# Narrow weights as the stationary side of three small projections in a two-layer decoder kernel

## The chip, the cores and the metric

The kernel runs on one core of one Trainium2 chip. The metric is the device time of one execution in microseconds (us), median of several runs. A change of about 0.2% (3.2 us) is what a measurement of this kernel can tell from no change.

## What is computed

Two decoder layers over 256 tokens of width 1024, all in float32. Layer 0 mixes with a forgetting attention, layer 1 with a gated sparse attention, and each is followed by a mixture of 64 experts. Three of its projections are narrow: they multiply the 256 normed and modulated tokens by a weight of 1024 x 16, 1024 x 48 or 1024 x 64.

```python
# forgetting attention, layer 0: 16 columns
log_f = jax.nn.log_sigmoid((proj[..., 3 * hd:] + b_f).astype(jnp.float32))
cum = jnp.cumsum(log_f, axis=1)
logits = logits + (cq.transpose(0, 2, 1)[..., None] - cum_k[:, :, None, :])
# sparse attention, layer 1: 48 columns
gates = jax.nn.sigmoid(proj[..., hd:] + b_gate).reshape(B, S, N_HEADS_B, 3)
o = gates[..., 0:1] * o_cmp + gates[..., 1:2] * o_sel + gates[..., 2:3] * o_win
# router, both layers: 64 columns
scores = jax.nn.sigmoid(jnp.matmul(h, w_router, preferred_element_type=jnp.float32))
_, top_e = lax.top_k(scores + b_router.astype(jnp.float32), TOP_K)
top_s = jnp.take_along_axis(scores, top_e, axis=-1)
top_w = top_s / jnp.sum(top_s, axis=-1, keepdims=True) * ROUTED_SCALE
```

## The kernel before

Each engine has its own list of instructions, written out by hand, and the lists meet at semaphores. SyncE streams all large weights, in units of 1 MiB, through a ring of 14 slots in a fixed order; it issues a unit when the slot's last user is done. TensorE works through the stages in order: the first conditioning vectors, the projections of layer 0 (`qkv`), its attention, the output projection (`out_a`), the experts of layer 0, then the key/value stage, the compression, the queries (`q`), the attention and the experts of layer 1. TensorE never skips ahead: an instruction that waits holds back all that stand behind it.

Before each projection, `pe_turn_rows` (L395) transposes the normed tokens (L404), and ScalarE and VectorE write the modulated tokens to `uT`, with the 1024 features in 8 chunks of 128 partitions and the 256 tokens along the row (L426, L434). `pe_modulated` (L410) waits for all eight chunks.

A normal projection unit (`pe_rows_unit`, L440) takes 128 tokens of `uT` as the stationary side and 256 weight columns as the moving side: 8 chunks times 2 token tiles are 16 matmuls. The three narrow projections do the same with 16, 48 or 64 moving columns:

```python
for t in range(NT):          # L865, the router; alike at L1379 and L1521
    for k in range(KC):
        mm = pe_.matmul(PS[:, Y0, t * N_EXP:(t + 1) * N_EXP], uT[:, k, t * P:(t + 1) * P],
                        w_router[:, k, :], start=(k == 0), stop=(k == KC - 1))
```

So each is 16 matmuls, and the result has tokens in partitions. A float32 matmul stands in the trace as two matmul records with a weight load each; a float32 transpose stands there as one.

- **Forget gate** (L1381). It is the first product of layer 0. VectorE's `forget_gate(step)` (L1701) and two ScalarE activations (Exp L1591, Ln L1594) turn it into log f, in five steps spread over the first units of the `qkv` loop (L1413). TensorE sums it over tokens after unit 2 (L1390 to L1392) and transposes the sums after unit 3 (L1398). `pe_rows_unit` of unit 0 (L446) stands right behind the forget matmuls.
- **Head gates** (L1523). The products of layer 1 ahead of the four `q` units (L446). VectorE adds the bias (L1854), ScalarE takes the sigmoid (L1667); the result is used after the queries.
- **Router** (L867, in `pe_moe`, both layers). Behind it stand `pe_gate` (L552, two matmuls of 512 columns that spread the layer's gate vector) and the shared expert's 32 matmuls (L875), then 16 transposes (L885), and only then the ranking (L890), which needs VectorE's mask of the chosen experts (L1066 to L1069). ScalarE takes the sigmoid of the scores from the PSUM accumulators (L1016).

Of the kernel before, what the change touches and what calls it, by code (L numbers as in the profile page):

```python
# [24 lines left out]
ALU = mybir.AluOpType  # L25
# [121 lines left out]
def build(nc, a, out):  # L147
    with ExitStack() as ctx:
# [40 lines left out]
        bias_f = sb("bias_f", [P, H])  # L189
        bias_gate = sb("bias_gate", [P, 3 * H])  # L190
# [7 lines left out]
        gates = sb("gates", [P, NT, 3 * H])  # L198
        small = sb("small", [P, 96])
# [62 lines left out]
        fg = [cut(F0 + 768 + 32 * i, [32]) for i in range(5)]  # L262
# [104 lines left out]
        ROUTING_SEMS = ["router_out", "scores_ready", "mask_ready", "ranks_out", "unranked_ready", "unranked_turned",  # L367
# [70 lines left out]
        KV_BANK = [0, 1, 2, 0, 1, 6]  # L438

# [351 lines left out]

        ranks_ps = PS[:, Y0 + 1, 0:NT * N_EXP].rearrange("p (t e) -> p t e", t=NT)
# [65 lines left out]
        def pe_moe(pe_, layer):  # L858
# [63 lines left out]
            pe_.wait_ge(routing["place_ready"], layer + 1)  # L922
            for kind in range(2):
# [86 lines left out]
        def act_moe(done, layer):  # L1010
# [5 lines left out]
            done(act.activation(scores.rearrange("p t e -> p (t e)"), PS[:, Y0, 0:NT * N_EXP], ACT.Sigmoid),  # L1016
                 routing["scores_ready"])
# [39 lines left out]
        def dve_moe(done, layer):  # L1057
# [7 lines left out]
            for t in range(NT):  # L1065
                done(dve.tensor_tensor(chosen_by[:, t, :], scores[:, t, :], bias_router[:, layer, :], ALU.add))  # L1066
# [3 lines left out]
            done(dve.tensor_tensor(scores, scores, routed, ALU.mult))  # L1070
# [194 lines left out]
        def _(pool):  # L1265
# [9 lines left out]
            for dst, src in ((gain_qa, "qnorm_a"), (gain_ka, "knorm_a"), (gain_qb, "qnorm_b"),  # L1275
                             (bias_f, "b_f_a"), (bias_gate, "b_gate_b")):
                pool.dma_start(dst[:, :], rows(a[src][0])).then_inc(params, 16)
            for i in range(3):
# [93 lines left out]
        def _(pe_):  # L1372
# [6 lines left out]
            for t in range(NT):  # L1379
                for k in range(KC):  # L1380
                    mm = pe_.matmul(PS[:, 6, t * H:(t + 1) * H], uT[:, k, t * P:(t + 1) * P], w_forget[:, k, :],  # L1381
                                    start=(k == 0), stop=(k == KC - 1))
            mm.then_inc(sem("forget_out"), 1)

            def forget_sums():
                lf = fg[4].rearrange("p (t h) -> p t h", t=NT)
                sums = PS[:, 6, 2 * H:4 * H].rearrange("p (t h) -> p t h", t=NT)
                pe_.wait_ge(sem("logf_ready"), 1)
# [24 lines left out]
            for j in range(12):  # L1413
# [107 lines left out]
            for t in range(NT):  # L1521
                for k in range(KC):
                    mm = pe_.matmul(PS[:, 6, t * 3 * H:(t + 1) * 3 * H], uT[:, k, t * P:(t + 1) * P],  # L1523
                                    w_gates[:, k, :], start=(k == 0), stop=(k == KC - 1))
            mm.then_inc(sem("gates_out"), 1)
# [36 lines left out]
        def _(act):  # L1562
# [21 lines left out]
            for j in range(8):  # L1584
# [4 lines left out]
                if j == 0:  # L1589
                    act.wait_ge(sem("forget_abs"), 1)  # L1590
                    done(act.activation(fg[2], fg[1], ACT.Exp, scale=-1.0), sem("forget_exp"))  # L1591
                elif j == 1:
                    act.wait_ge(sem("forget_1p"), 1)
                    done(act.activation(fg[3], fg[2], ACT.Ln), sem("forget_ln"))  # L1594
# [71 lines left out]
            act.wait_ge(sem("gates_biased"), 1)  # L1666
            done(act.activation(gates[:, :, :], gates[:, :, :], ACT.Sigmoid), sem("gates_ready"))  # L1667
# [15 lines left out]
        def _(dve):  # L1683
# [15 lines left out]
            z, az, ez, lnz, logf = fg  # L1699

            def forget_gate(step):  # L1701
                if step == 0:
                    dve.wait_ge(sem("forget_out"), 1)
                    done(dve.tensor_tensor(z.rearrange("p (t h) -> p t h", t=NT),
                                           PS[:, 6, 0:2 * H].rearrange("p (t h) -> p t h", t=NT),
                                           bias_f[:, :].unsqueeze(1).to_broadcast([P, NT, H]), ALU.add))
                    done(dve.tensor_scalar(az, z, -1.0, None, ALU.mult))
                    done(dve.tensor_tensor(az, az, z, ALU.max), sem("forget_abs"))
                elif step == 1:
                    dve.wait_ge(sem("forget_exp"), 1)  # L1710
                    done(dve.tensor_scalar(ez, ez, 1.0, None, ALU.add), sem("forget_1p"))
                    done(dve.tensor_scalar(z, z, 0.0, None, ALU.min))
                elif step == 2:
                    dve.wait_ge(sem("forget_ln"), 1)
                    done(dve.tensor_tensor(logf, z, lnz, ALU.subtract), sem("logf_ready"))
                elif step == 3:
                    dve.wait_ge(sem("cum_out"), 1)
# [282 lines left out]
```

## Time and profile before

| | |
|---|---|
| median of 3 runs | 1584.86 us |
| range of these runs | 1583.45 to 1586.05 us |
| the profiled execution | 1586.27 us, span 1584.4 us, clock 0.957 |
| TensorE (PE) busy | 1480.9 us, 93% |
| VectorE (DVE) busy | 417.6 us, 26% |
| ScalarE (ACT) busy | 280.8 us, 18% |
| moved by DMA | 512.38 MB, mean 323 GB/s |

The span runs from the first to the last instruction; the execution's own time is 1.9 us longer. PE busy counts matmuls, PEld weight loads, which run beside them. PEclk is the TensorE clock that was granted, as a share of 2.4 GHz: 1.00 is 2.4 GHz, 0.50 is 1.2 GHz. "Idle before" names what an engine waited for.

### The profile page before, as it was taken

What the parts mean: (1) busy time and instruction counts of PE and PEld (TensorE: products, weight loads), DVE (VectorE), ACT (ScalarE), POOL (GpSimd) and SP (SyncE); (2) the same over time, 40 slices, a digit from 0 to 9 for tenths busy, and PEclk for the clock granted to TensorE, in tenths of its full rate; (3) what the DMA queues carried; (4) which work ended last, traced back from release to release, by engine and by line L of the source; (5) the groups of instructions that cost most, each with busy time, mean ns of one, the idle gap of its engine ahead of it and who ended that gap; (6) DMA issues with size and microseconds to landing.
All of it is one profiled execution on the core that took longest, in us unless ns stands there. A gap on an engine that the chain in (4) does not pass through costs nothing.

```text
span 1584.4 us, 21198 instructions
## 1 busy us (share of the span) xinstructions
PE 1480.9 (93%) x8561; PEld 888.8 (56%) x8561; DVE 417.6 (26%) x969; ACT 280.8 (18%) x549; POOL 31.4 (2%) x81
## 2 busy tenths in 40 slices
PE   4999988999999999999798868789999999999998
PEld 2777777644555444454376757676455454544443
DVE  0466432111111111111367247522111111111111
ACT  2211332111111111111212215421111111111110
POOL 4000001000000000000000000001000000000000
PEclk9999987999999999999999768889999999999999
DMA  9967602399999999999999810031999999999996
GB/s 342 413 265 309 255 27 87 135 376 422 421 421 422 374 421 420 421 420 422 417 404 384 360 53 1 1 113 34 368 421 422 421 420 375 422 420 421 420 421 264
DMA packets 71315, 512.38 MB, mean 323 GB/s; under 512 B 8176, under 2 KB 8400, under 8 KB 9264
## 3 DMA queue, kind: packets, MB, share of 16 engines
q1 hardware_dynamic: 69984, 508.59, 78.5%
q0 software_dynamic: 800, 1.28, 0.4%
q8 instruction: 69, 1.13, 0.3%
q10 hardware_dynamic: 432, 1.13, 0.2%
q14 instruction: 30, 0.25, 0.0%
HBM read 509.92 MB, written 1.05 MB: 322 GB/s over the span
## 4 chain that ended last, share of the span: by engine, by line
PE 87%; DVE 5%; ACT 3%; issue 2%; DMA 1%; DVEq 0%; ACTq 0%
PE PS L823 23%; PE PS L446 13%; PE PS L813 12%; PE PS L831 12%; PE PS L846 11%; PE PS L875 2%; PE PS L616 2%; PE PS L404 2%; PE PS L469 2%; PE PS L483 1%; DMA h<-in_x 1%; PE PS L913 1%; PE PS L867 1%; DVE acc L527 1%; PE PS L586 1%
## 5 line engine op out<-in xcount | busy, mean ns | idle before, releaser
L823 PE MATMUL PS<-ring,scratch 128*32 128x512 f32 (+2 forms) x2048 | 367.8, 594 | 1.4 <-ACT scratch L1030 1.4
L823 PEld LDWEIGHTS PS<-ring,scratch 128*32 128x32 f32 (+2 forms) x2048 | 118.8, 127 | 243.7 <-issue 241.9
L446 PE MATMUL PS<-ring,uT 128*128 128x256 f32 x960 | 224.3, 395 | 2.9 <-ACT uT L417 1.8
L813 PEld LDWEIGHTS PS<-scratch,u 128*128 128x128 f32 x1664 | 190.8, 192 | 39.5 <-issue 37.6
L446 PEld LDWEIGHTS PS<-ring,uT 128*128 128x128 f32 x960 | 189.2, 199 | 31.8 <-ACT uT L417 2.6
L813 PE MATMUL PS<-scratch,u 128*128 128x128 f32 x1664 | 199.6, 278 | 1.4 <-ACT scratch L1030 1.4
L1154 DVE TENSOR_TENSOR scratch<-PS,gate_row 128x512 f32<-128x512 f32 x104 | 72.0, 692 | 464.1 <-PE PS L831 464.1
L831 PE MATMUL PS<-ring,scratch 128*32 128x512 f32 (+2 forms) x1024 | 189.3, 596 | 1.2 <-DVE item_first_i L1139 1.2
L846 PE MATMUL PS<-scratch 128*128 128x512 f32 x416 | 187.3, 593 | 0.0
L1038 ACT ACTIVATE scratch<-PS 128x256 f32<-128x256 f32 x52 | 20.0, 384 | 675.7 <-PE PS L823 675.7
L831 PEld LDWEIGHTS PS<-ring,scratch 128*32 128x32 f32 (+2 forms) x1024 | 56.8, 126 | 125.5 <-issue 123.8
L846 PEld LDWEIGHTS PS<-scratch 128*128 128x128 f32 x416 | 75.0, 190 | 76.3 <-issue 74.6
L1147 DVE TENSOR_TENSOR scratch<-scratch,PS 128x256 f32<-128x256 f32 x52 | 21.9, 422 | 337.5 <-ACT scratch L1038 337.5
L1030 ACT ACTIVATE scratch<-PS 128x512 f32<-128x512 f32 x104 | 62.1, 597 | 162.9 <-PE PS L813 162.9
L527 DVE SCALAR_TENSOR_TENSOR acc<-ring,cond,acc 128x256 f32<-128x256 f32 x168 | 81.5, 485 | 6.0
L483 PE MATMUL PS<-ring,scratch 128*32 128x256 f32 x512 | 42.5, 460 | 12.2 <-DVE scratch L1687 6.8
L616 PE MATMUL PS<-scratch,uT 128*128 128x65 f32 x288 | 38.4, 284 | 12.2 <-ACT uT L639 12.2
L616 PEld LDWEIGHTS PS<-scratch,uT 128*128 128x128 f32 x288 | 35.0, 196 | 19.3 <-ACT uT L639 17.3
L404 PE MATMUL PS<-ident,u 128*128 128x128 f32 x112 | 25.2, 419 | 18.4 <-ACT u L721 16.1
L647 ACT ACTIVATE scratch<-scratch,stats 128x128 f32<-128x128 f32 (+1 forms) x96 | 35.7, 443 | 19.0 <-DVE stats L666 19.0
L469 PE MATMUL PS<-four_rows,acc 128*128 128x1 f32 x128 | 22.8, 283 | 15.1 <-ACT acc L497 14.8
L404 PEld LDWEIGHTS PS<-ident,u 128*128 128x128 f32 x112 | 22.9, 227 | 20.4 <-issue 17.7
(306 smaller groups left out, 918.6 us busy)
## 6 DMA issues: line engine op xcount, KB each, us to landing
ring<-in_w_exp SPq DMA_DIRECT2D x384, 1024.0 KB, 15.5
ring<-in_w_ada_units SPq DMA_DIRECT2D x56, 1024.0 KB, 11.7
ring<-in_w_in_a_units SPq DMA_DIRECT2D x12, 1024.0 KB, 8.5
ring<-in_w_cmp_units SPq DMA_DIRECT2D x8, 1024.0 KB, 9.4
ring<-in_w_sh_units SPq DMA_DIRECT2D x6, 1024.0 KB, 16.2
ring<-in_w_kv_b_units SPq DMA_DIRECT2D x6, 1024.0 KB, 19.6
ring<-in_w_o_a_units SPq DMA_DIRECT2D x4, 1024.0 KB, 7.2
ring<-in_w_in_b_units SPq DMA_DIRECT2D x4, 1024.0 KB, 17.1
```

The lines of the kernel that those rows point to most:

```text
L404: mm = pe_.transpose(PS[:, b, (k % 2) * SEQ + t * P:(k % 2) * SEQ + (t + 1) * P], src[:, t, k * P:(k + 1) * P], ident[:, :])
L446: mm = pe_.matmul(PS[:, bank, t * UC:(t + 1) * UC], lhs[:, k, t * P:(t + 1) * P], w[:, k, :], start=(k == 0), stop=(k == KC - 1))
L469: return [pe_.matmul(PS[:, ADA_COLUMNS, c0 + c:c0 + c + 1], part[:, c * P:(c + 1) * P], rows, start=True, stop=True) for c in range(2)]
L483: mm = pe_.matmul(PS[i:i + 32, ada_parts_bank(j), 0:UC], cond_cols[:, k, :], w[:, k, :], start=(k < 4), stop=(k >= 4))
L527: done(dve.scalar_tensor_tensor(out=sums, in0=w[:, k, :], scalar=cond[:, k:k + 1], in1=sums, op0=ALU.mult, op1=ALU.add), ada_products_read ...
L616: mm = pe_.matmul(PS[:, 6 + b % 2, hd * (DH + 1):(hd + 1) * (DH + 1)], pT[:, n * P:(n + 1) * P], values(br, kt, 4 * g + hd), start=(kt == ...
L813: mm = pe_.matmul(PS[:, bank, i * w:(i + 1) * w], u[:, t, k * P:(k + 1) * P], hot[:, t, :], start=(t == 0), stop=(t == NT - 1))
L823: mm = pe_.matmul(PS[i * w:(i + 1) * w, GU, :], x[:, kk, i * w:(i + 1) * w], gate_and_up, start=(kk == 0), stop=(kk == KC - 1))
L831: mm = pe_.matmul(PS[i * w:(i + 1) * w, Y0 + half, :], hT[:, j, i * w:(i + 1) * w], down[:, j, half * 512:(half + 1) * 512], start=(j == 0 ...
L846: mm = pe_.matmul(OUT[t][:, half * 512:(half + 1) * 512], hot_wT[0:rows, t * P:(t + 1) * P], y_rows[0:rows, half * 512:(half + 1) * 512], ...
L1030: act.activation(x_pair[g % 2][:, 4 * half:4 * half + 4, :].rearrange("p k s -> p (k s)"), PS[:, gather_bank(g, half), :], ACT.Copy).then_ ...
L1154: dve.tensor_tensor(y_rows[:, half * 512:(half + 1) * 512], PS[:, Y0 + half, :], gate_row[:, half * 512:(half + 1) * 512], ALU.mult).then_ ...
```

## The change

The three narrow projections swap sides: each chunk of the narrow weight is stationary and all 256 tokens move, so that 8 matmuls stand in place of 16, and the result has the 16, 48 or 64 features in partitions and tokens along the row. Bias, sigmoid and log-sigmoid work in that layout, and two small transposes per projection bring the finished result back to tokens in partitions. The biases of the two gates are loaded as columns. For the router the transposed scores are read from PSUM by VectorE.

```diff
+        def pe_narrow(pe_, w, bank, lhs, columns, turned):
+            for k in range(KC):
+                mm = pe_.matmul(PS[0:columns, bank, 0:SEQ], w[:, k, :], lhs[:, k, :], start=(k == 0), stop=(k == KC - 1))
+            mm.then_inc(turned, 1)
+        def pe_narrow_rows(pe_, src, rows):
+            for t in range(NT):
+                mm = pe_.transpose(rows[:, t, :], src[:, t * P:(t + 1) * P], ident[0:src.shape[0], 0:src.shape[0]])
+            return mm
...
-            for t in range(NT):
-                for k in range(KC):
-                    mm = pe_.matmul(PS[:, Y0, t * N_EXP:(t + 1) * N_EXP], uT[:, k, t * P:(t + 1) * P],
-                                    w_router[:, k, :], start=(k == 0), stop=(k == KC - 1))
-            mm.then_inc(routing["router_out"], 1)
+            pe_narrow(pe_, w_router, Y0, uT, N_EXP, routing["router_out"])
             pe_gate(pe_, 2 * layer + 1)
+            pe_.wait_ge(routing["sigmoids"], layer + 1)
+            pe_narrow_rows(pe_, narrow_T[E64, :], scores_ps).then_inc(routing["scores_ready"], 1)
...
-            done(act.activation(scores.rearrange("p t e -> p (t e)"), PS[:, Y0, 0:NT * N_EXP], ACT.Sigmoid),
-                 routing["scores_ready"])
+            done(act.activation(narrow_T[E64, :], PS[E64, Y0, 0:SEQ], ACT.Sigmoid), routing["sigmoids"])
...
+            def forget_turn():
+                pe_.wait_ge(sem("logf_ready"), 1)
+                pe_narrow_rows(pe_, logits_f, narrow_rows(6, SEQ, H)).then_inc(sem("logf_turned"), 1)
...
                 if j == 2:
+                    forget_turn()
+                elif j == 3:
                     forget_sums()
-                elif j == 3:
+                elif j == 4:
                     forget_rows()
...
             for j in range(4):
                 pe_rows_unit(pe_, AT["q", j], j, uT)
+                if j == 0:
+                    pe_.wait_ge(sem("gates_active"), 1)
+                    pe_narrow_rows(pe_, narrow_T[0:3 * H, :], narrow_rows(6, SEQ, 3 * H)).then_inc(sem("gates_turned"), 1)
...
-            act.wait_ge(sem("gates_biased"), 1)
-            done(act.activation(gates[:, :, :], gates[:, :, :], ACT.Sigmoid), sem("gates_ready"))
+            act.wait_ge(sem("gates_out"), 1)
+            done(act.activation(narrow_T[0:3 * H, :], PS[0:3 * H, 6, 0:SEQ], ACT.Sigmoid, bias=bias_gate[:, :]),
+                 sem("gates_active"))
...
-                    done(dve.tensor_scalar(az, z, -1.0, None, ALU.mult))
-                    done(dve.tensor_tensor(az, az, z, ALU.max), sem("forget_abs"))
+                    done(dve.tensor_scalar(logits_f, PS[0:H, 6, 0:SEQ], bias_f[:, :], None, ALU.add))
+                    done(dve.scalar_tensor_tensor(out=softplus_f, in0=logits_f, scalar=-1.0, in1=logits_f,
+                                                  op0=ALU.mult, op1=ALU.max), sem("forget_abs"))
...
+                elif step == 3:
+                    dve.wait_ge(sem("logf_turned"), 1)
+                    done(dve.tensor_copy(logf_rows, PS[:, 6, SEQ:SEQ + NT * H]), sem("logf_copied"))
```

TensorE's list at the router, before. `router_loaded` is the weight's DMA, `modulated_*` the eight chunks of `uT`, `slot_loaded` a unit of the ring:

```order
L404 MATMUL PS<-ident,u 128x128 x15
L867 MATMUL PS<-scratch,uT 128x64 [waits router_loaded,modulated_dve,modulated_act]
L867 MATMUL PS<-scratch,uT 128x64 x15
L552 MATMUL PS<-scratch,ones 128x512 [waits gate_diag_ready]
L552 MATMUL PS<-scratch,ones 128x512
L875 MATMUL PS<-uT,ring 128x256 [waits slot_loaded6]
L875 MATMUL PS<-uT,ring 128x256 x7
```

And now, with the line numbers of the changed kernel (L445 is the narrow matmul, L453 the transpose back, L568 the gate, L890 the shared expert):

```order
L406 MATMUL PS<-ident,u 128x128 x15
L445 MATMUL PS<-uT,scratch 64x256 [waits router_loaded,modulated_dve,modulated_act]
L445 MATMUL PS<-uT,scratch 64x256 x7
L568 MATMUL PS<-scratch,ones 128x512 [waits gate_diag_ready]
L568 MATMUL PS<-scratch,ones 128x512
L453 MATMUL PS<-ident,narrow_T 128x64 [waits sigmoids]
L453 MATMUL PS<-ident,narrow_T 128x64
L890 MATMUL PS<-uT,ring 128x256 [waits slot_loaded6]
L890 MATMUL PS<-uT,ring 128x256 x7
```

Eight matmuls stand in place of 16, and behind the gate TensorE now waits for ScalarE's sigmoids ahead of two transposes; the shared expert is queued behind that wait.

TensorE's list at the head gates, now:

```order
L406 MATMUL PS<-ident,u 128x128 x15
L445 MATMUL PS<-uT,w_gates 48x256 [waits cmp_v_read,modulated_dve,modulated_act]
L445 MATMUL PS<-uT,w_gates 48x256 x7
L462 MATMUL PS<-ring,uT 128x256 [waits slot_loaded1]
L462 MATMUL PS<-ring,uT 128x256 x15
L453 MATMUL PS<-ident,narrow_T 128x48 [waits gates_active]
L453 MATMUL PS<-ident,narrow_T 128x48
L462 MATMUL PS<-ring,uT 128x256 [waits slot_loaded2]
```

Here the wait stands behind the first `q` unit of 16 matmuls (L462 now, L446 before).

## Rows read from the trace of the kernel before

**Rows 1.** The page: span, busy time, and the chain by engine

```profile
span 1584.4 us, 21198 instructions
...
PE 87%; DVE 5%; ACT 3%; issue 2%; DMA 1%; DVEq 0%; ACTq 0%
```

**Rows 2.** Waits: who waited for whom, us in total, times, longest us

```profile
SPq L1215 <- PE PS L831: 432.1, 48, 10.4
SPq L1215 <- PE PS L446: 260.6, 14, 112.2
```

**Rows 3.** Timeline, TensorE, forget gate: start us, us, engine line op, count [idle before]

```profile
42.27 3.65 PE L404 MATMUL PS<-ident,u 128*128 128x128 f32 x16
47.06 6.98 PE L1381 MATMUL PS<-w_forget,uT 128*128 128x16 f32 x32 [1.14 <-ACT uT L426]
53.89 9.08 PE L446 MATMUL PS<-ring,uT 128*128 128x256 f32 x32
62.90 1.07 PE L483 MATMUL PS<-ring,scratch 128*32 128x256 f32 x16
```

**Rows 4.** Timeline, TensorE, 58 to 62.9 us

```profile
57.44 5.53 PE L446 MATMUL PS<-ring,uT 128*128 128x256 f32 x24
```

**Rows 5.** Timeline, TensorE, router of layer 0 and shared expert

```profile
256.98 3.65 PE L404 MATMUL PS<-ident,u 128*128 128x128 f32 x16 [4.83 <-ACT u L721]
261.76 7.06 PE L867 MATMUL PS<-scratch,uT 128*128 128x64 f32 x32 [1.14 <-ACT uT L426]
268.61 3.73 PE L552 MATMUL PS<-scratch,ones 128*128 128x512 f32 x4
272.13 14.34 PE L875 MATMUL PS<-uT,ring 128*128 128x256 f32 x64
286.31 1.91 PE L885 MATMUL PS<-ident,uT 128*128 128x128 f32 x16
288.05 0.33 PE L890 MATMUL PS<-scratch,before 128*128 128x64 f32 x2
```

**Rows 6.** Timeline, TensorE, router of layer 1 and shared expert

```profile
1064.46 7.06 PE L867 MATMUL PS<-scratch,uT 128*128 128x64 f32 x32 [1.14 <-ACT uT L426]
1071.31 3.73 PE L552 MATMUL PS<-scratch,ones 128*128 128x512 f32 x4
1074.83 14.05 PE L875 MATMUL PS<-uT,ring 128*128 128x256 f32 x64
1088.72 1.47 PE L885 MATMUL PS<-ident,uT 128*128 128x128 f32 x12
```

**Rows 7.** Timeline, TensorE, head gates and the four q units

```profile
885.06 5.04 PE L1523 MATMUL PS<-w_gates,uT 128*128 128x48 f32 x32 [1.14 <-ACT uT L426]
889.91 29.92 PE L446 MATMUL PS<-ring,uT 128*128 128x256 f32 x128
```

**Rows 8.** Timeline, TensorE, spreading of the compressed heads in layer 1

```profile
940.93 7.19 PE L1545 MATMUL PS<-scratch 64*128 64x512 f32 x8 [0.53 <-ACT scratch L1675]
```

**Rows 9.** Windows, TensorE: stretch, its us, PE busy (x), PEclk, DMA share, GB/s

```profile
54.00:57.90 3.90, 3.90 (x11) 1.00 1.01 416
...
884.00:887.20 3.20, 2.14 (x20) 1.00 1.00 417
887.30:893.80 6.50, 6.50 (x23) 0.50 1.01 420
...
261.80:268.60 6.80, 6.80 (x32) 0.50 0.01 2
268.80:272.60 3.80, 3.80 (x7) 0.50 0.01 2
273.10:286.00 12.90, 12.90 (x61) 1.00 0.25 83
...
941.00:948.00 7.00, 7.00 (x8) 0.50 0.00 0
```

**Rows 10.** Timeline, ScalarE and VectorE, behind the router of layer 0

```profile
268.86 0.28 ACT L1016 ACTIVATE scratch<-PS 128x128 f32<-128x128 f32 x1 [6.72 <-PE PS L867]
...
270.93 0.29 DVE L1069 TENSOR_TENSOR scratch<-scratch 128x128 f32<-128x128 f32 x1
```

**Rows 11.** Groups by line and shape: busy us, mean ns | idle before

```profile
L1038 ACT ACTIVATE scratch<-PS 128x256 f32<-128x256 f32 x26 | 10.0, 384 | 337.9 <-PE PS L823 337.9
...
L527 DVE SCALAR_TENSOR_TENSOR acc<-ring,cond,acc 128x256 f32<-128x256 f32 x168 | 81.5, 485 | 6.0
```

More of the change, by code:

```diff
@@ L261, in build @@
         forget_queries = cut(F0 + 512, [SEQ])
-        fg = [cut(F0 + 768 + 32 * i, [32]) for i in range(5)]
+        logf_rows = cut(F0 + 768, [NT * H])
+        logits_f, softplus_f = narrow_T[0:H, :], cut(S0 + 2304, [SEQ])[0:H]
         def of_queries(rows):
@@ L922, in pe_moe @@
             pe_.wait_ge(routing["place_ready"], layer + 1)
+            pe_.wait_ge(routing["raw_scores_read"], layer + 1)
             for kind in range(2):
@@ L1378, in _ @@
             pe_.wait_ge(params, 16 * N_PARAMS)
[L1379 to L1383, printed above, removed]
+            pe_narrow(pe_, w_forget, 6, uT, H, sem("forget_out"))
+            def forget_turn():
+                pe_.wait_ge(sem("logf_ready"), 1)
+                pe_narrow_rows(pe_, logits_f, narrow_rows(6, SEQ, H)).then_inc(sem("logf_turned"), 1)
             def forget_sums():
-                lf = fg[4].rearrange("p (t h) -> p t h", t=NT)
-                sums = PS[:, 6, 2 * H:4 * H].rearrange("p (t h) -> p t h", t=NT)
-                pe_.wait_ge(sem("logf_ready"), 1)
+                lf = logf_rows.rearrange("p (t h) -> p t h", t=NT)
+                sums = narrow_rows(6, SEQ + NT * H, H)
+                pe_.wait_ge(sem("logf_copied"), 1)
                 pe_.wait_ge(consts, 1)
@@ L1520, in _ @@
             pe_.wait_ge(sem("cmp_v_read"), 1)
[L1521 to L1525, printed above, removed]
+            pe_narrow(pe_, w_gates, 6, uT, 3 * H, sem("gates_out"))
             for j in range(4):
                 pe_rows_unit(pe_, AT["q", j], j, uT)
+                if j == 0:
+                    pe_.wait_ge(sem("gates_active"), 1)
+                    pe_narrow_rows(pe_, narrow_T[0:3 * H, :], narrow_rows(6, SEQ, 3 * H)).then_inc(sem("gates_turned"), 1)
             pe_turn_rows(pe_, q_rows, (sem("q_normed"), 4), "q")
@@ L1713, in forget_gate @@
                 elif step == 2:
                     dve.wait_ge(sem("forget_ln"), 1)
-                    done(dve.tensor_tensor(logf, z, lnz, ALU.subtract), sem("logf_ready"))
+                    done(dve.scalar_tensor_tensor(out=logits_f, in0=logits_f, scalar=0.0, in1=softplus_f,
+                                                  op0=ALU.min, op1=ALU.subtract), sem("logf_ready"))
                 elif step == 3:
+                    dve.wait_ge(sem("logf_turned"), 1)
+                    done(dve.tensor_copy(logf_rows, PS[:, 6, SEQ:SEQ + NT * H]), sem("logf_copied"))
+                elif step == 4:
@@ L1717, in forget_gate @@
                     dve.wait_ge(sem("cum_out"), 1)
-                    sums = PS[:, 6, 2 * H:4 * H].rearrange("p (t h) -> p t h", t=NT
-                                                           ).unsqueeze(2).to_broadcast([P, NT, 2, H])
+                    sums = narrow_rows(6, SEQ + NT * H, H).unsqueeze(2).to_broadcast([P, NT, 2, H])
                     done(dve.tensor_copy(of_queries(cum), sums))
                     done(dve.tensor_scalar(of_keys(cum_keys), sums, -1.0, None, ALU.mult), sem("cum_ready"))
-                elif step == 4:
+                elif step == 5:
@@ L1988 @@
                                      given["norm_ffn"][1], given["c"])
-    for name in ("x", "positions", "b_f_a", "qnorm_a", "knorm_a", "pe_cmp_k", "pe_cmp_v", "w_cmp_k2", "w_cmp_v2",
-                 "knorm_b", "b_gate_b", "qnorm_b", "b_router"):
+    for name in ("x", "positions", "qnorm_a", "knorm_a", "pe_cmp_k", "pe_cmp_v", "w_cmp_k2", "w_cmp_v2",
+                 "knorm_b", "qnorm_b", "b_router"):
         laid_out[name] = given[name]
+    laid_out["b_f_column"] = given["b_f_a"].reshape(H, 1)
+    laid_out["b_gate_column"] = given["b_gate_b"].reshape(3 * H, 1)
     for name, value in laid_out.items():
```

35 lines of the change are left out of this document (17 added, 18 removed).

## The prediction

> **What bounds the kernel now.** I read the page first. TensorE makes up 87% of the chain that ended last, and issue, DMA and the other engines share the rest [rows 1]. So what TensorE's list loses, the kernel loses, unless a load is late. The waits say that it is not: the queue that loads the weights waited for TensorE, 432 us behind the expert matmuls and 261 us behind the projections [rows 2]. Around the router DMA moves nearly nothing, since the ring is full there (share 0.01 [rows 9]). After it, loads and matmuls both follow from this point, so a gain ahead of the experts moves the whole rest and is not given back to DMA. The same holds at the forget gate and the head gates, where TensorE waited for `uT` and for no load [rows 3, 7].
>
> Then I read TensorE's own timeline at the four places, from start to start. Forget gate: 53.89 - 47.06 = 6.83 us, and the unit behind it 9.01 us [rows 3]. Router of layer 0: 6.85 us, gate 3.52 us, shared expert 14.18 us [rows 5]; of layer 1: 6.85, 3.52 and 13.89 us [rows 6]. Head gates: 4.85 us, the four `q` units about 29.9 us [rows 7].
>
> **Two levels of the clock.** The length of a matmul depends on the clock, so the windows come next. Layer 0's router and gate ran at a granted clock of 0.50, which is 1.2 GHz; from 273 us it was 1.00 [rows 9]. At the head gates it was 1.00 until 887.2 us and then 0.50 until about 894, so the first `q` unit paid for it. The column is no guide at the forget gate. It reads 1.00, but the first 8 records of 256 columns behind it took (57.44 - 53.89)/8 = 0.44 us each, and the later 24 took 5.46/24 = 0.23 [rows 3, 4]. The gate's 512-column records give 3.52/4/2 = 0.44 us for 256 columns at 0.50 [rows 5]. At the full clock it is 13.89/64 = 0.217 us [rows 6]. So the first 11 us of layer 0's products start at the low level as well.
>
> **What the change does to the narrow matmuls.** Before, 16 matmuls are 32 records, each with a 128-column weight load and at most 64 moving columns, so the load sets their pace: 6.85/32 = 0.214 us at the low clock [rows 5] and 4.85/32 = 0.152 us at the mostly full clock [rows 7]. Now 8 matmuls are 16 records with 256 moving columns. That is 16 x 0.44 = 7.0 us low and 16 x 0.217 = 3.5 us full. So at the low level nothing is gained, although half of the matmuls are gone, and at the full level 1.4 us of 4.85 are.
>
> The Trainium skill, page "TensorE: Matmul & The Clock Gate", section "LDWEIGHTS (loading the stationary operand)", gives P/1.2 ns for P columns, which is 107 ns for 128. By that, an estimate, the 32 loads of before take 3.4 us, as long as the 16 new records, and the swap gains nothing even at the full clock. The 0.152 us of the head gates stands against it, and the row decides.
>
> **What the low clock does.** Everything hangs on whether the narrow matmuls bring the clock up or keep it up. Two rows of the same length stand against each other. The gate's records (128 rows and 128 columns of the array, 512 moving columns) began at the low level at 268.6 and 1071.3 us, and the clock was up some 4 us later [rows 5, 6, 9]. L1545 is as dense, 8 records of 0.90 us, but fills 64 of the 128 rows; after 7.2 us of it the clock still read 0.50 [rows 8, 9]. The new matmuls use all 128 rows, but 16, 48 or 64 columns. No row shows columns left empty at the low level without neighbours beside them. I take the nearest row, L1545, which also leaves at least half of the array unused. So in my forecast the narrow matmuls do not raise the clock, and gate and shared expert behind them come as before.
>
> **The sum.** Forget gate 7.04 - 6.83 = +0.2 us. Each router 7.04 - 6.85 = +0.2. Head gates: full until 887.2 us, 2.14/0.217 = 10 records, then 6 x 0.44 = 2.6, together 4.8 against 4.85: 0. The `q` units then pay for the low stretch as before. Bounds of a narrow block: 3.5 us (all full) and 7.0 us (all low).
>
> Transposes back, two at each of four places: a record costs 1.91/16 = 0.12 us at the full clock [rows 5] and 3.65/16 = 0.23 low [rows 3]. Forget gate and head gates full, 0.24 each; the routers low, right behind the gate, 0.46 each: +1.4 us. Bounds: 1.0 us in all if all are full, and 1.4 + 4 x 0.8 = 4.6 us if TensorE had to wait for every ScalarE answer.
>
> That answer is costed at nothing. ScalarE began 0.25 us after the last router matmul and took 0.28 us [rows 5, 10]; with 256 columns it is 0.38 [rows 11], so the sigmoids are there some 0.8 us after the narrow matmuls, under the gate's 3.5 us (1.7 at full clock). At the head gates the first `q` unit of 7 us covers it, at the forget gate a whole unit. Without that cover it costs up to 0.8 us a place, and the shared expert waits with it. Behind the router, VectorE's choice now starts up to 4 us later than before. Its mask was begun at 270.9 us and is needed at 288.0, so the shared expert covers that. If it did not, the ranking would be late next [rows 5, 10].
>
> VectorE's forget steps now work on 256 columns instead of 32, up to 0.49 us each [rows 11], with one step more, and sums and transposed sums come one unit later. All of it lies beside units of 9 to 10 us with eight units to come: 0, and 0.5 us where VectorE is the later one. The bias loads, the same number in smaller pieces, land long before 47 us: 0.
>
> Total: 0.2 + 0.2 + 0.2 + 0 + 1.4 = **+2.0 us**. Against the profiled execution that is 1586.3 + 2.0 = 1588.3 us. That execution lies 1.4 us over the median of 1584.86, so I forecast **1586.9 us**, within what can be told from no change.
>
> **Rival A, the narrow matmuls wake the clock (as L552 does).** Then the low stretch of about 4 us starts with them: 9 records of 0.44 and 7 of 0.217 are 5.5 us, and all behind is at the full clock. Forget gate: 5.5 + 32 x 0.217 = 12.4 against 15.84, -3.4 us. Router of layer 0: 5.5 + 1.74 + 13.89 = 21.1 against 24.55, -3.4; of layer 1 against 24.26, -3.1. Head gates: the clock never falls, 3.5 + 27.8 = 31.3 against 34.75, -3.5. All transposes at the full clock, +1.0. Together -12.4: 1572.5 us by the median. For it: L552, and that all 128 rows stream without a gap. Against it: L1545. The Trainium skill's page just named, section "The HAM clock gate (the "warmup" mystery)", says that activity releases the throttle and names no share of the array; by it this rival would be the forecast. Rows 8 do not follow it in that short form. Chance 38%. In between, with later rises, it gives -7 us.
>
> **Rival B, slower: the clock is already down when the head gates start.** Before, it was 1.00 at their start and fell 2 us in [rows 9]. If it is low at 885 us, the 16 records take 7.04 instead of 4.85 us, +2.2 us. If it also rises 4 us later in the `q` units, 9 records lose 0.22 each, +2.0. With the +2.0 of the forecast that is +6.2, 1591.1 us. It decides as soon as no high stretch reaches the head gates. For it: those matmuls use 48 of 128 columns, and the clock did fall in this place. Against it: the transposes ahead of them are untouched, and the clock came up behind those. Chance 8%.
>
> **Rival C, only the head gates gain.** Started at the full clock, 256 columns in a row may hold a level that they cannot raise: 4.85 - 3.5 = 1.4 us and about 1.9 us in the `q` units, against +2.0 elsewhere: -1.3, 1583.6 us. Still no change. Chance 7%.
>
> **How the numbers follow.** The forecast's own case has 47%, its own range 1584 to 1589.5 us: the transposes' bounds and the clock's falls elsewhere, such as one more or fewer low stretch of 1.7 us. Rival A lies at 1569 to 1577. The range must hold both: 1571 to 1589.5, which leaves out rival B, the low end of A and the high end of the waits. Faster by over 0.2% (3.2 us): A and some 3% of the others, 41%. Slower by over 0.2%: B and the forecast's case with stalls, 15%. Within 0.2%: 44%.
>
> **What would show it.** Forecast right: the narrow blocks at router and forget gate take 7 us, the gate behind the router still 3.5 us at 0.50, and the first `qkv` unit still about 9 us. Rival A: narrow blocks near 5.5 us, gate 1.7 us, first `qkv` unit 7 us, and no fall at the head gates. Any wait of the shared expert for the sigmoids shows a cost I set to nothing; so does VectorE's mask as the releaser of the ranking.

## Result and profile after

The changed kernel took 1575.4 us (median of 6 runs, 1571.4 to 1580.3), the kernel before 1584.6 us in the same job (6 runs, 1583.5 to 1586.1). The ratio is 0.9942, 95% interval 0.9923 to 0.9962: 9.2 us less, faster by more than 0.2%. The forecast of no change was wrong. The time lies in the range, near the 1572.5 us of rival A. The profiled execution of the changed kernel took 1571.4 us, the least of its six, and is 14.7 us shorter than that of before.

The page of the changed kernel, span and chain [rows 1]:

```profile
span 1569.7 us, 21088 instructions
...
PE 87%; DVE 6%; ACT 4%; issue 2%; DMA 1%; DVEq 0%; ACTq 0%
```

The mix of the chain is nearly the same, so the time went inside TensorE's own list. TensorE's timeline of the changed kernel at the four places, in the columns of [rows 3]. L445 is the narrow block, L462 a unit of 32 records, L568 the gate, L453 the transposes back, L890 the shared expert:

```profile
44.23 3.61 PE L445 MATMUL PS<-uT,w_forget 128*16 128x256 f32 x16 [1.14 <-ACT uT L428]
47.77 7.17 PE L462 MATMUL PS<-ring,uT 128*128 128x256 f32 x32
...
82.29 0.29 PE L453 MATMUL PS<-ident,narrow_T 16*128 16x16 f32 x2
...
249.14 3.65 PE L406 MATMUL PS<-ident,u 128*128 128x128 f32 x16 [4.83 <-ACT u L737]
253.93 5.46 PE L445 MATMUL PS<-uT,scratch 128*64 128x256 f32 x16 [1.14 <-ACT uT L428]
259.32 1.98 PE L568 MATMUL PS<-scratch,ones 128*128 128x512 f32 x4
261.24 0.34 PE L453 MATMUL PS<-ident,narrow_T 64*128 64x64 f32 x2
261.50 14.08 PE L890 MATMUL PS<-uT,ring 128*128 128x256 f32 x64
...
874.93 5.56 PE L445 MATMUL PS<-uT,w_gates 128*48 128x256 f32 x16 [1.14 <-ACT uT L428]
880.42 7.17 PE L462 MATMUL PS<-ring,uT 128*128 128x256 f32 x32
887.53 0.32 PE L453 MATMUL PS<-ident,narrow_T 48*128 48x48 f32 x2
```

Against [rows 3, 5, 7]: the forget gate's block fell from 6.83 to 3.54 us and the unit behind it from 9.01 to 7.11. The router's block went from 6.85 to 5.39 and the gate from 3.52 to 1.92. The head gates' block became longer, 5.49 instead of 4.85, but the first unit behind it is at full pace. Windows of the changed kernel show the clock under these blocks. Here and in the windows below the columns are the stretch, its us, the busy us (and instructions) of PE, PEld, DVE, ACT and POOL, then PEclk, DMA share and GB/s:

```profile
254.00:257.40 3.40, 3.40 (x9) 1.83 (x10) 0.96 (x1) 0.29 (x1) 0.00 (x0) 0.50 0.02 5
257.60:259.30 1.70, 1.70 (x8) 0.82 (x6) 0.00 (x0) 0.00 (x0) 0.00 (x0) 0.99 0.00 0
...
874.90:878.80 3.90, 3.87 (x10) 1.90 (x11) 0.00 (x0) 0.82 (x1) 0.00 (x0) 0.50 1.01 420
879.00:880.40 1.40, 1.40 (x7) 0.62 (x5) 0.00 (x0) 0.00 (x0) 0.00 (x0) 1.00 1.03 421
```

Both blocks began at 0.50 (1.2 GHz) and ended at 1.00 (2.4 GHz): 64 and 48 filled columns of the array did bring the clock up, during the block itself. That is rival A, and what the forecast ruled out.

Where the 14.7 us of the two profiles lie, from starts in TensorE's timeline. "Turn" is where a block's transposes of `u` begin:

| stretch | before, us | after, us | difference |
|---|---|---|---|
| start to forget gate | 47.06 | 44.23 | -2.8 |
| forget gate and first unit | 15.84 | 10.65 | -5.2 |
| to the turn that ends layer 0's attention | 152.8 | 155.6 | +2.8 |
| to the router block | 46.1 | 43.4 | -2.6 |
| router, gate, shared expert, layer 0 | 24.55 | 21.49 | -3.1 |
| experts, to the turn of layer 1 | 495.8 | 495.8 | 0 |
| to the head gates | 102.9 | 103.7 | +0.8 |
| head gates and `q` units | 38.9 | 38.0 | -0.9 |
| layer 1's attention | 94.6 | 93.1 | -1.5 |
| to the router block | 45.8 | 46.2 | +0.4 |
| router, gate, shared expert, layer 1 | 24.26 | 21.69 | -2.6 |
| rest | 495.7 | 495.8 | +0.1 |

The four changed places gave 11.8 us. The start gave 2.8 us that no step of the prediction names. The attention stages moved by -1.5 and +2.8 us, although the change puts nothing there but the forget gate's small steps beside the `qkv` units. Over the twelve profiles of this study that add nothing to it, layer 0's stretch took from 152.8 to 156.2 us, with old and with new blocks alike. The expert stages kept their time, so nothing was given back to DMA, as argued from [rows 2].

### The profile page after: what moved, and what is told of

Same layout as the page of the kernel before. It is cut to its first block, busy times and chain, and to the rows that moved or that the text cites. A ratio compares the mean times of both kernels' runs of the same rounds, so it can differ in the third digit from the quotient of the medians.

```text
span 1569.7 us, 21088 instructions
## 1 busy us (share of the span) xinstructions
PE 1467.1 (93%) x8505; PEld 868.6 (55%) x8505; DVE 423.5 (27%) x968; ACT 281.7 (18%) x549; POOL 31.5 (2%) x81
## 4 chain that ended last, share of the span: by engine, by line
PE 87%; DVE 6%; ACT 4%; issue 2%; DMA 1%; DVEq 0%; ACTq 0%
PE PS L840 23%; PE PS L462 13%; PE PS L830 12%; PE PS L848 12%; PE PS L863 11%; PE PS L632 2%; PE PS L890 2%; PE PS L406 2%; PE PS L485 1%; DVE acc L543 1%; PE PS L445 1%; PE PS L499 1%; DMA h<-in_x 1%; PE PS L928 1%; PE PS L619 1%
## 5 line engine op out<-in xcount | busy, mean ns | idle before, releaser
L462 PE MATMUL PS<-ring,uT 128*128 128x256 f32 x960 | 220.5, 390 | 3.1 <-ACT uT L419 1.9
L462 PEld LDWEIGHTS PS<-ring,uT 128*128 128x128 f32 x960 | 186.0, 196 | 31.7 <-ACT uT L419 2.6
L1053 ACT ACTIVATE scratch<-PS 128x256 f32<-128x256 f32 x52 | 19.9, 383 | 675.7 <-PE PS L840 675.7
## 6 DMA issues: line engine op xcount, KB each, us to landing
ring<-in_w_exp SPq DMA_DIRECT2D x384, 1024.0 KB, 15.6
```

What stands on the lines that cost most here:

```text
L462: mm = pe_.matmul(PS[:, bank, t * UC:(t + 1) * UC], lhs[:, k, t * P:(t + 1) * P], w[:, k, :], start=(k == 0), stop=(k == KC - 1))
```

## The experiments

All ratios are to the kernel before, run beside it on the same chip, with 95% intervals. A "low stretch" is one in which the granted clock was 0.50.

**The three places one by one.** Each kernel swaps one place alone and leaves the others as before. The edit, shown for the forget gate (the other two are cut out of the diff above in the same way):

```diff
-            for t in range(NT):
-                for k in range(KC):
-                    mm = pe_.matmul(PS[:, 6, t * H:(t + 1) * H], uT[:, k, t * P:(t + 1) * P], w_forget[:, k, :],
-                                    start=(k == 0), stop=(k == KC - 1))
-            mm.then_inc(sem("forget_out"), 1)
+            pe_narrow(pe_, w_forget, 6, uT, H, sem("forget_out"))
...
```

> Only the forget gate swaps sides; router and head gates are as before. Theory A (a dense stream of 256 columns through all 128 rows wakes the clock, however few columns of the array the weight fills): the narrow block takes 5.5 us where the clock is low at its start and 3.5 us where it is not, the first qkv unit 7.0 instead of 9.0 us, so 3.2 to 5.2 us faster than before. Theory B (my forecast: a weight of 16 columns does not wake it): the block takes 7.0 us, the unit 9.0 us, and the time is the same within 0.5 us. By theory A a narrow block is faster in some runs than in others, so the runs spread wider than those of before.

Measured: 1583.8 us, 12 runs, ratio 0.9992 (0.9979 to 1.0005).

> Only the head gates swap sides. Theory A: the clock no longer falls in the q units; 31.3 us instead of 34.75 us for gates and q units where the clock is up at their start (-3.3 us with the transposes), 33.5 us where it first has to rise (-1 us). Theory B: 4.8 us for the gates, the q units as before, 0.2 us slower.

Measured: 1582.3 us, 9 runs, ratio 0.9976 (0.9966 to 0.9986).

> Only the router swaps sides, in both layers. Theory A: narrow block 5.5 us, gate 1.8 to 1.9 us, shared expert 13.9 us in each layer, 3.0 us a layer and 6 us in all faster than before. Theory B: 7.0, 3.5 and 14.2 us, 1.3 us slower in all.

Measured: 1588.9 us, 12 runs, ratio 1.0015 (1.0001 to 1.0028).

And the whole change again in the same job:

> The whole change once more. If its parts act alone (theory A), the gain is the sum of those of the other three kernels of this job, within 1.5 us. If the profiled run of the change shown so far (the fastest of its six) owed its 14.7 us to where the clock rose and fell, this profile shows the same narrow blocks but other stretches of low clock elsewhere, and its gain lies near 9 us.

Measured: 1577.0 us, 6 runs, ratio 0.9937 (0.9922 to 0.9952).

Each place did locally what rival A says. TensorE's timeline of the forget gate alone:

```profile
47.49 3.61 PE L445 MATMUL PS<-uT,w_forget 128*16 128x256 f32 x16 [1.14 <-ACT uT L428]
51.03 7.17 PE L462 MATMUL PS<-ring,uT 128*128 128x256 f32 x32
```

and of the head gates alone:

```profile
884.50 3.62 PE L444 MATMUL PS<-uT,w_gates 128*48 128x256 f32 x16 [1.14 <-ACT uT L427]
...
895.16 0.32 PE L452 MATMUL PS<-ident,narrow_T 48*128 48x48 f32 x2
895.41 20.99 PE L461 MATMUL PS<-ring,uT 128*128 128x256 f32 x96
```

Forget gate with first unit: 10.65 us instead of 15.84. Head gates with `q` units up to the next turn: 36.1 us instead of 38.9, and here the block began at the full clock and no fall came. The router alone took 2.9 us off layer 0 (26.5 instead of 29.3 us from the turn to the end of the shared expert) and 2.7 off layer 1, and the kernel was still no faster than before: 3.3 us slower by the medians, with an interval that just leaves out no change. The three parts come to 1583.8 - 1585.7, 1582.3 - 1585.7 and 1588.9 - 1585.7: -1.9, -3.4 and +3.3 us, together -2.0, where the whole gives -8.7. **The parts do not add up.** Of the 6.7 us between them 2.8 belong to the start, which only the whole change moves: the forget block began at 46.9 to 47.5 us in the profiles of the three parts and at 44.3 in that of the whole. The remaining 3.9 us are hardly more than the intervals of the four ratios allow together (some 4 us, an estimate from their widths). The router alone is the clear case: 5.6 us gained at its two places, and none in the total.

**What moves is the clock elsewhere.** In the router-only profile the gains are lost in stages that the edit does not touch. Layer 1's attention took 101.1 us instead of 94.6, the head gates with `q` 40.8 instead of 38.9 (their block began low and took 6.83 us), layer 0's attention 156.1 instead of 152.8. The next pair asks whether the place of the work in time alone does this. One kernel is before with 0.55 us of unused matmuls behind layer 0's shared expert. The other is router-only with 2.86 us of them at that point, meant to let the rest of the program start as late as in before. The edit of the second:

```diff
+        def pe_keep_busy(pe_, n, bank=7, columns=248):
+            for _ in range(n):
+                pe_.matmul(PS[:, bank, 264:264 + columns], ones[:, :], causal[:, 0:columns], start=True, stop=True)
...
+            if layer == 0:
+                pe_keep_busy(pe_, 6)
+                pe_keep_busy(pe_, 1, columns=228)
```

> The kernel before, with 0.55 us of extra matmuls (332 columns, results unused) behind the shared expert of layer 0 and nothing else changed. In the router-only kernel the attention of layer 1 ran with a low stretch of the clock from 974.75 to 991.75 us and took 101.1 us from the end of the queries to its end, against 94.65 us before. Theory A (the low stretches depend on where a stage falls against the clock's own rhythm, and a gain upstream only moves them): moving all that follows by a fraction of a microsecond changes the time by other than 0.55 us, by 3 to 7 us where it brings the attention into the same position. Theory B (the swap itself harms something in the router-only kernel): 0.5 to 0.6 us slower than before, and the attention takes 94.7 us.

Measured: 1588.9 us, 11 runs, ratio 1.0013 (1.0003 to 1.0023), which is 2.5 us over before by the medians and 0.5 to 3.6 us by the interval.

> The router-only kernel, with 2.86 us of extra matmuls at the same place, so that all that follows starts where it does before the change. Theory A: the low stretch in the attention of layer 1 is gone, and although work was added the kernel is faster than the router-only one (1588.9 us), by 6.5 - 2.9 = 3.6 us or so. Theory B: 2.9 us slower than the router-only kernel.

Measured: 1583.5 us, 12 runs, ratio 0.9987 (0.9975 to 0.9999), with 2.9 us more work 5.4 us less than router-only by the medians (4.4 by the ratios, since the two come from two jobs). Windows of layer 1's attention, first router-only, then router-only with the added matmuls:

```profile
922.80:1023.90 101.10, 82.97 (x490) 67.71 (x490) 63.06 (x152) 42.16 (x92) 0.00 (x0) 0.71 0.00 1
974.80:991.70 16.90, 16.90 (x85) 15.40 (x86) 10.80 (x27) 6.82 (x15) 0.00 (x0) 0.50 0.00 1
```

```profile
922.70:1017.30 94.60, 75.13 (x491) 60.48 (x491) 63.02 (x152) 42.25 (x92) 0.00 (x0) 0.77 0.00 1
974.80:991.70 16.90, 15.34 (x138) 13.36 (x138) 15.60 (x39) 11.79 (x28) 0.00 (x0) 1.00 0.00 1
```

The same 490 matmuls start 0.1 us apart in the two profiles. With the clock at 0.50 between 974.8 and 991.7 us, 85 of them were done in that stretch, with it at 1.00, 138. That one low stretch is the 6.5 us. So this stage, in which TensorE is about 80% busy, has low stretches whose number changes although it starts at the same microsecond of the program. The second profile of the whole change has such a one, too, where the first took 93.1 us:

```profile
916.30:1017.50 101.20, 81.69 (x490) 66.29 (x490) 63.06 (x151) 42.70 (x92) 0.00 (x0) 0.72 0.00 1
```

This answers the question of the pair, and the answer is no: the place in time, counted from the program's start, does not decide alone. What is shown is that 2.86 us of added work left the router-only kernel faster, by 4.4 us by the ratios, whose intervals just part. Why is not shown. Its profile starts the rest 0.3 us earlier than the router-only one, in spite of the added work, because layer 0's attention had taken 3.3 us less ahead of it, so a part of the gain need not be the added matmuls' doing. For before with 0.55 us added, the attention kept its 94.7 us, and the loss came at the head gates, which began low (40.9 instead of 38.9 us). Its interval reaches down to the 0.55 us themselves, so it does not show that a small shift costs more than itself.

**Rows or columns.** This kernel is before, with the gate's four matmuls reading 64 rows instead of 128, as L1545 does:

```diff
+            rows = slice(0, 64 if i in (1, 3) else P)
-                mm = pe_.matmul(PS[:, half, :], ones[:, :],
-                                gate_diag[:, 4 * half:4 * half + 4, :].rearrange("p k c -> p (k c)"),
+                mm = pe_.matmul(PS[:, half, :], ones[rows, :],
+                                gate_diag[rows, 4 * half:4 * half + 4, :].rearrange("p k c -> p (k c)"),
```

> The kernel before, where the gate matmuls of both routers (L552) use 64 of 128 rows; half of the gate vector is left out of the output. If the filled rows decide whether a dense stream brings the clock up (my reading of L1545 against L552), the clock stays at 0.50 through the gate and comes up only some 4 us into the shared expert, which then takes 15.5 to 16 us instead of 13.9 to 14.2. If rows do not matter, gate and shared expert read as before, and something else kept the clock down behind L1545.

Measured: one run of 1622.4 us. This kernel leaves half of the gate vector out, so layer 1 routes otherwise, and the total says nothing. TensorE's timeline at the routers of both layers, and windows at that of layer 0:

```profile
270.12 3.78 PE L553 MATMUL PS<-scratch,ones 64*128 64x512 f32 x4
273.83 15.78 PE L876 MATMUL PS<-uT,ring 128*128 128x256 f32 x64
...
1072.26 3.78 PE L553 MATMUL PS<-scratch,ones 64*128 64x512 f32 x4
1075.97 15.78 PE L876 MATMUL PS<-uT,ring 128*128 128x256 f32 x64
```

```profile
270.20:273.80 3.60, 3.60 (x4) 1.09 (x4) 2.81 (x14) 0.28 (x1) 0.00 (x0) 0.50 0.01 2
274.00:277.20 3.20, 3.20 (x8) 2.57 (x9) 0.01 (x1) 1.02 (x1) 2.03 (x1) 0.50 0.00 0
277.50:289.40 11.90, 11.90 (x57) 10.46 (x56) 0.00 (x0) 1.88 (x2) 2.36 (x2) 1.00 0.26 89
```

With all rows the clock was up some 4 us after the gate began [rows 5, 9]. With half of them it stayed at 0.50 through the gate and 3.4 us into the shared expert, 7.1 us after the gate began, and the shared expert took 15.6 instead of 14.2 us. Layer 1's router repeats it: 15.6 instead of 13.9 us. So in these runs rows left empty kept a dense matmul from raising the clock, as at L1545, and columns left empty did not. L1545 was a good row, for another question. Only half of the rows was tried, no other share.

**Holding the clock up.** If the low stretches are the price, unused matmuls in front of the places should take it away. First the changed kernel with 10 of them ahead of each router's transposes and 14 ahead of layer 1's first ones, where TensorE waited anyhow:

```diff
+            pe_keep_busy(pe_, 10, 3)
             pe_.wait_ge(mix_added, 4)
...
```

> The changed kernel, with unused matmuls where TensorE waits ahead of the transposes: 10 of 248 columns (4.1 us) ahead of both routers and 14 (5.8 us) ahead of the key/value stage. If the dense stream through all rows is what brings the clock up, it never falls there: transposes 1.9 instead of 3.65 us (with about 1 us of that given back to the modulation of the tokens), narrow block 3.5 instead of 5.5, gate 1.7 instead of 1.9: 3 us a router, 1 us at the key/value stage, 6 to 7 us faster than the change, save for what the attention's low stretches take or give by their new position (up to 7 us either way).

Measured: 1564.5 us, 5 runs, ratio 0.9854 (0.9840 to 0.9867), 11 us under the change by the medians of two jobs and 13 to 14 by the ratios, where 6 to 7 was expected. One part of the miss is the stretch from the turn of layer 1 to the head gates: 99.7 instead of 103.7 us, where 1 us was expected. TensorE's timeline at layer 0's router, and then at the forget gate, where nothing was added:

```profile
251.74 1.94 PE L410 MATMUL PS<-ident,u 128*128 128x128 f32 x16 [0.65 <-ACT u L741]
254.85 3.64 PE L449 MATMUL PS<-uT,scratch 128*64 128x256 f32 x16 [1.17 <-ACT uT L432]
258.42 1.98 PE L572 MATMUL PS<-scratch,ones 128*128 128x512 f32 x4
```

```profile
44.45 5.89 PE L449 MATMUL PS<-uT,w_forget 128*16 128x256 f32 x16 [1.14 <-ACT uT L432]
50.27 7.17 PE L466 MATMUL PS<-ring,uT 128*128 128x256 f32 x32
```

Transposes 1.94 instead of 3.65 us, narrow block 3.57, gate 1.9. The forget gate's block took 5.82 us here, the unit behind it 7.11. Windows inside the block show the pace of the records. The clock's column reads 1.00 at this place in any case, as in [rows 9], so the pace must tell the level:

```profile
44.50:48.50 4.00, 4.00 (x10) 1.37 (x11) 3.36 (x11) 0.00 (x0) 0.00 (x0) 1.00 1.02 426
...
49.20:50.20 1.00, 1.00 (x6) 0.29 (x3) 0.70 (x2) 0.00 (x0) 0.00 (x0) 1.00 0.99 410
```

Some 0.44 us a record at first and 0.22 at the end (10.4 x 0.44 + 5.6 x 0.22 = 5.8): 16 filled columns woke the clock as well.

Then such matmuls in all the waits that had low stretches (2 a step of the compression, ahead of the `q` transposes and of the compressed probabilities, one a batch of both attentions), in the changed kernel and in before:

> The kernel with unused matmuls ahead of routers and key/value stage, and more of them where TensorE waits in the compression (2 a step), ahead of the queries' transposes (9), ahead of the compressed probabilities (11) and once in each batch of both attentions that reads two key tiles. If a dense stream holds the clock: no low stretch from 870 us to the end, some 4 us less at the compressed heads, 2 us each at the transposes and the compressed logits, no low stretch in either attention. 1553 us, give or take 5, and runs within 3 us of each other, since there is nothing left whose position matters.

Measured: 1553.8 us, 5 runs, ratio 0.9784 (0.9768 to 0.9800). This is the best kernel of the study, 32 us under before. Two parts of the expectation failed: the runs lie 6.1 us apart, not within 3, and the profile still has low stretches behind 870 us, of some 7 us at 909 and 10 us at 933 and 991.

> The same unused matmuls in the kernel before. With the clock held up in the attentions, the change's own gain is left: 1.4 us for each of four narrow blocks, 2.8 us at the load of x, less 1.0 us of transposes, and at the forget gate and the head gates what the old narrow matmuls cost by letting the clock fall (up to 2 us each). So 6 to 11 us slower than the same with the change. If the gain of the change lies in the attention's low stretches alone, the two are within 2 us.

Measured: 1562.0 us, 7 runs, ratio 0.9841 (0.9829 to 0.9854). So with the clock mostly held up in both, the change is worth 8.2 us, about what it gives without. The two profiles lie 15.8 us apart, but this one was the slowest of its seven runs. The two kernels show what the old block does by itself. TensorE's timeline at the head gates and windows of that place and of layer 1's router, in before with the added matmuls:

```profile
875.39 4.82 PE L1532 MATMUL PS<-w_gates,uT 128*128 128x48 f32 x32 [1.14 <-ACT uT L430]
```

```profile
875.50:877.50 2.00, 2.00 (x19) 2.00 (x20) 0.00 (x0) 0.68 (x1) 0.00 (x0) 1.00 0.97 406
878.00:880.00 2.00, 2.00 (x11) 2.00 (x11) 0.00 (x0) 0.00 (x0) 0.00 (x0) 0.50 1.00 414
1049.70:1051.60 1.90, 1.90 (x18) 1.90 (x18) 1.01 (x1) 0.83 (x1) 0.00 (x0) 1.00 0.00 0
1052.00:1054.00 2.00, 2.00 (x11) 2.00 (x11) 0.00 (x0) 0.00 (x0) 0.00 (x0) 0.50 0.00 0
```

and of the same head gates in the changed kernel with the added matmuls, its timeline:

```profile
866.78 3.65 PE L449 MATMUL PS<-uT,w_gates 128*48 128x256 f32 x16 [1.23 <-ACT uT L432]
870.37 7.17 PE L466 MATMUL PS<-ring,uT 128*128 128x256 f32 x32
```

The three old blocks of head gates and routers, now begun at 1.00, lost the clock 2.2 to 2.6 us in. In the new form all three kept it. From block to `q` turn, 38.9 against 36.1 us. From router block to the end of the shared expert, 22.5 against 19.7 in both layers.

**The first 2.8 us.** In the changed kernel `x` is there sooner, and TensorE's first blocks start sooner with it. ScalarE's timeline, first of before, then of the changed kernel:

```profile
19.29 1.06 ACT L691 ACTIVATE u<-h 128x1024 f32<-128x1024 f32 x1 [11.39 <-DMA h<-in_x]
```

```profile
16.80 1.06 ACT L707 ACTIVATE u<-h 128x1024 f32<-128x1024 f32 x1 [8.88 <-DMA h<-in_x]
```

Ahead of it both kernels do the same but for the two biases, which were loaded spread over 128 partitions (8 and 24 KB) and are now columns of 0.1 and 0.2 KB. The experiment loads both spread again, unused, beside the columns:

```diff
+        bias_f_rows = sb("bias_f_rows", [P, H])
+        bias_gate_rows = sb("bias_gate_rows", [P, 3 * H])
...
+                             (bias_f_rows, "b_f_a"), (bias_gate_rows, "b_gate_b")):
```

> The changed kernel, which also loads the two biases the old way, spread over 128 partitions, into tiles that nothing reads. In all three profiles with both biases as columns the tokens x landed so that ScalarE began at 16.7 to 16.9 us and the forget matmuls at 44.2 to 44.5 us; in all others, with one or both spread, at 19.2 to 19.9 and 46.9 to 47.6 us. Theory A (the spread loads of a few bytes hold up the load of x): 19.2 to 19.9 and 47 us again, 2.8 us slower than the change, save for what the attention's low stretches do. Theory B (luck of the runs): 16.8 and 44.3 us, no slower.

Measured: 1579.2 us, 6 runs, ratio 0.9949 (0.9931 to 0.9967). `x` was read from 18.31 us:

```profile
18.31 1.06 ACT L709 ACTIVATE u<-h 128x1024 f32<-128x1024 f32 x1 [10.41 <-DMA h<-in_x]
```

Over all profiles: 16.5 to 16.9 us in the five whose kernels have both biases as columns, 19.2 to 19.9 in the eight that have one or both of them spread, 18.3 in this one. So the spread loads delay `x`, by 1.5 us of 2.5 here, in one profile. By what they delay it, the rest of the 2.5 us, and why one of the two alone already costs all of it, stay open. The times do not settle it: 1579.2 against 1575.4 and 1577.0 us, in intervals that overlap.

**The sigmoid's answer.** Here the router's transposes back stand ahead of the gate, so the gate no longer covers ScalarE:

```diff
-            pe_gate(pe_, 2 * layer + 1)
             pe_.wait_ge(routing["sigmoids"], layer + 1)
             pe_narrow_rows(pe_, narrow_T[E64, :], scores_ps).then_inc(routing["scores_ready"], 1)
+            pe_gate(pe_, 2 * layer + 1)
```

> The changed kernel, with the router's transposes back ahead of the gate matmuls, so that nothing covers ScalarE's sigmoids. TensorE waits about 0.8 us in each layer (0.25 us to start, 0.38 us of work, 0.2 us back); the clock stays up, since 0.8 us is short. 1.6 us slower by its own count, and by the attention's position up to 7 us either way. If the cover was not needed, the shared expert starts 2.2 us after the narrow block's end as in the change.

Measured: 1574.6 us, 5 runs, ratio 0.9923 (0.9911 to 0.9936). Two waits are too short to show in the time, whose interval overlaps that of the change. TensorE's timeline shows the wait at layer 0's router, 0.47 us and not 0.8:

```profile
262.12 0.34 PE L453 MATMUL PS<-ident,narrow_T 64*128 64x64 f32 x2 [0.47 <-ACT narrow_T L1032]
```

## Why the prediction was wrong

**The step that failed** is "I take the nearest row, L1545 (...) So in my forecast the narrow matmuls do not raise the clock". L1545 leaves half of the rows empty, the new matmuls leave columns empty, and I treated the two as one. The gate on 64 rows and the blocks at 253.93 and 874.93 us part them: in these runs half of the rows empty kept the clock down, empty columns did not, down to 16 filled of 128. The Trainium skill's sentence, page "TensorE: Matmul & The Clock Gate", section "The HAM clock gate (the "warmup" mystery)", that activity releases the throttle, gave the right forecast here. The trace agrees with it for columns (the block at 253.93 us began at 0.50 and ended at 1.00). The gate on 64 rows, busy for 3.7 us at 0.50 with the clock still down behind it, does not follow it in that short form, nor does the old router block, busy for 6.85 us at 0.50 [rows 5, 9].

**A second step was wrong and hid the mechanism:** "0.152 us at the mostly full clock", and that the row decides against the Trainium skill's 107 ns. 0.152 is a mean over two levels. [Rows 9] hold the parts: 2.14 us for 20 records at 1.00, which is 0.107 each, and the other 12 at 0.50 took (889.91 - 887.20)/12 = 0.23. So at the full clock the row confirms the 107 ns of the Trainium skill, page "TensorE: Matmul & The Clock Gate", section "LDWEIGHTS (loading the stationary operand)". At 0.50 a record takes twice that, 0.214 us [rows 5]. At one and the same level the swap gains nothing: 32 x 0.107 = 3.4 us against 3.54 at the full clock, 6.85 against 7.04 by my estimate at the low one. All of its gain is the clock: the old block never raised it (6.8 to 7.0 us in every profile where it began low) and lost it where it began high (4.4 to 5.4 us; 1.7 to 2.6 us in, where the clock's column can tell), the new one raised it (5.3 to 5.8 us) or kept it (3.5 to 3.6).

**Rival A, term by term.** Forget gate -5.2 us instead of -3.4, since the block found the clock up at its start (3.54, not 5.5). It did so in four of the seven profiles that have the new block there, and began low in three (5.7 to 5.8 us). The old block began high there in three of seven, so this is a coin that falls ahead of the change, and some 2 of the 5.2 us are luck. At like starts block and first unit take 10.65 us new against 13.98 old when high, and 12.8 to 12.9 against 15.6 to 16.2 when low. Routers -3.1 and -2.6 with their transposes, forecast -3.4 and -3.1 without 0.25 for them: right. Head gates -0.9 instead of -3.5, since the block of this profile began low, as rival B had it. Its own condition held (it "decides as soon as no high stretch reaches the head gates"), its price did not, because the block then woke the clock itself: 38.0 us, where the old block begun low takes 40.8. Begun high, in the head gates alone, it gave -2.8. Together -11.8 in this profile, forecast -12.4. That the median, -9.2, lies near it as well is partly luck: the 2.8 us of the start and the high start of the forget gate stand against the low start of the head gates and low stretches elsewhere.

**The other terms.** Transposes back: 0.22 to 0.27 us each, all at the full clock, 1.0 us in all, rival A's value. The sigmoid costed at nothing: right. ScalarE had them at 259.81 us and the gate ran until 261.24. The mask had time: VectorE ended its choice at 267.7 us, and TensorE began the ranking at 277.2 us straight behind its transposes. VectorE's forget steps: no wait of TensorE for them, 0 as said. **Bias loads "land long before 47 us": 0** was wrong. I asked whether they are late, not whom they delay: the load of `x`, which came 2.5 us sooner with the columns, 1.5 us of it by them in the one profile that tests it. And the clock's falls elsewhere, "such as one more or fewer low stretch of 1.7 us", were sized too small: one such stretch is worth up to 6.5 us in layer 1's attention. Such stretches can be why the change's runs spread over 9 us, and why the medians differ by 9.2 us where the profiles differ by 14.7: the second profile of the change, its job's slowest run, has one, the first has not. The kernel before has them too: its six runs here spread over 2.6 us, but its 27 and 23 runs in two later jobs over 7.2 and 8.5.

Left open: what decides whether a low stretch falls into a stage. The place in time alone does not. The losses of router-only are read from one profile, whose time is its median.

## What to carry to other kernels

Before you price a matmul by its mean, split it by the granted clock. Here a block of short, load-paced matmuls let the clock fall, and the same product with the narrow weight stationary and 256 columns moving raised it, at no saving of its own. Ask what a row of the trace leaves empty before you take it as a model: here filled rows counted, and filled columns did not. Where the clock is part of the gain, a local gain can be missing from the total, as for the router alone. It may help to compare parts in a kernel whose clock is held up, which was done here for the whole change only. The unused matmuls in the waits were worth more than the change itself (22 us by the medians on top of it).

## What the runs showed that was not expected

- Matmuls of 64 filled rows left the clock at 0.50 for 7.1 us where those of 128 rows had it up some 4 us after they began. 64, 48 or 16 filled columns did as well as 128.
- With 2.86 us of added work the router-only kernel was 4.4 us faster. Layer 1's attention began within 0.1 us of the same time in both profiles and took 94.6 us in one and 101.1 in the other.
- Two biases of 8 and 24 KB, spread over 128 partitions and loaded from another queue, go with a load of 1 MB that is read some 2.5 us later.
